# The shift products of five seams in a one-core encoder kernel: 16 matmuls with the shift stationary, the last squares added on VectorE, and the reciprocal root spread at another place

## The reference

```python
def rms_norm(x, gain=None):
    y = x * lax.rsqrt(jnp.mean(x * x, axis=-1, keepdims=True) + EPS)
    return y if gain is None else y * gain
def modulate(h, shift, scale):
    return h * (1 + scale[:, None, :]) + shift[:, None, :]
for i in range(DEPTH):
    mod = cond @ mod_w[i] + mod_b[i]
    sh1, sc1, g1, sh2, sc2, g2, sh3, sc3, g3 = jnp.split(mod, 9, axis=-1)
    x = x + 0.5 * g1 * swiglu(modulate(rms_norm(x), sh1, sc1), ffn1_w_gu[i], ffn1_w_down[i])
    x = x + g2 * mixer(modulate(rms_norm(x), sh2, sc2))
    x = x + 0.5 * g3 * swiglu(modulate(rms_norm(x), sh3, sc3), ffn2_w_gu[i], ffn2_w_down[i])
    x = rms_norm(x, post_gain[i])
```

## Time and profile before

| | us |
|---|---|
| three runs | 2045.1, 2045.5, 2046.54 (median 2045.5) |
| the profiled execution | 2046.44 |
| its span, first to last instruction | 2044.6 |
| PE busy | 2006.3 (98%), 9341 matmul records |
| DVE busy | 1117.0 (55%) |
| ACT busy | 702.6 (34%) |
| POOL busy | 185.3 (9%) |
| mean granted TensorE clock | 0.995 of full |

### The profile page before, as it was taken

The page is one execution under the profiler, slowest core; times in us unless marked ns, Lnnn a source line. Parts: engine busy times, 40 slices in busy tenths (PEclk is TensorE's granted clock), DMA queues, the critical chain, the costliest instruction groups (busy, mean ns, idle before and its releaser), DMA issues.

```text
span 2044.6 us, 23873 instructions
## 1 busy us (share of the span) xinstructions
PE 2006.3 (98%) x9341; PEld 1667.2 (82%) x9341; DVE 1117.0 (55%) x1712; ACT 702.6 (34%) x1025; POOL 185.3 (9%) x216
## 2 busy tenths in 40 slices
PE   6999999999999999999999999999999999999998
PEld 4888888888888888888888888878888888888886
DVE  7664653689757655636763552465455474333334
ACT  5222322454643222225321222345454443222122
POOL 3110100016600101000110000000000000000000
PEclk9999999999999999999999999999999999999999
DMA  8665542322025655623453542221221132322321
GB/s 318 238 209 182 187 146 84 98 86 73 21 91 197 206 173 196 189 85 96 154 196 123 181 139 91 82 94 53 73 72 63 52 93 93 112 92 85 103 87 57
DMA packets 72015, 253.99 MB, mean 124 GB/s; under 512 B 8025, under 2 KB 8153, under 8 KB 71938
## 3 DMA queue, kind: packets, MB, share of 16 engines
q1 hardware_dynamic: 53280, 185.62, 27.9%
q0 software_dynamic: 18512, 67.26, 9.9%
q10 hardware_dynamic: 146, 0.09, 0.0%
HBM read 250.70 MB, written 2.10 MB: 124 GB/s over the span
## 4 chain that ended last, share of the span: by engine, by line
PE 92%; DVE 5%; ACT 1%; issue 1%; POOL 1%; DMA 0%; DVEq 0%; ACTq 0%; SPq 0%; POOLq 0%
PE bank L1244 29%; PE bank L1249 28%; PE bank L1245 28%; PE bank L1308 1%; DVE arena L1067 1%; DVE wlo L711 1%; DVE top L1066 1%; PE bank L1653 1%; PE bank L1695 1%; PE bank L1584 1%; PE bank L1426 1%; ACT whi L397 1%; PE bank L1428 1%; PE bank L1427 1%; PE bank L1641 0%
## 5 line engine op out<-in xcount | busy, mean ns | idle before, releaser
L1244 PE MATMUL bank<-h_hi,whi 128*128 128x512 f32 x1808 | 720.6, 399 | 9.0 <-DVE wlo L711 4.7
L1245 PE MATMUL bank<-h_hi,wlo 128*128 128x512 f32 x1808 | 708.3, 392 | 0.0
L1249 PE MATMUL bank<-h_lo,whi 128*128 128x512 f32 x1808 | 596.0, 392 | 1.7 <-DVE h_lo L828 1.2
L397 ACT ACTIVATE whi<-wraw 128x1024 fp32r<-128x1024 f32 x338 | 347.2, 1054 | 266.9 <-PE bank L1249 263.9
L711 DVE TENSOR_TENSOR wlo<-wraw,whi 128x1024 fp32r<-128x1024 f32 x325 | 390.5, 1224 | 55.0 <-ACT whi L397 53.6
L1244 PEld LDWEIGHTS bank<-h_hi,whi 128*128 128x128 f32 x1808 | 342.5, 189 | 79.1 <-issue 5.6
L1249 PEld LDWEIGHTS bank<-h_lo,whi 128*128 128x128 f32 x1808 | 341.1, 189 | 75.1 <-DVE h_lo L828 2.2
L1245 PEld LDWEIGHTS bank<-h_hi,wlo 128*128 128x128 f32 x1808 | 342.5, 189 | 66.4
L1249 PE MATMUL bank<-hid_lo,whi 128*128 128x512 f32 x832 | 324.7, 390 | 3.2 <-DVE hid_lo L904 3.2
L1244 PE MATMUL bank<-hid_hi,whi 128*128 128x512 f32 x832 | 325.0, 391 | 0.0
L1245 PE MATMUL bank<-hid_hi,wlo 128*128 128x512 f32 x832 | 324.2, 390 | 0.0
(11 more groups left out here) (232 smaller groups left out, 1418.4 us busy)
## 6 DMA issues: line engine op xcount, KB each, us to landing
wraw<-in_w_units_dram SPq DMA_DIRECT2D x306, 512.0 KB, 3.5
arena<-in_mod_t_dram POOLq DMA_DIRECT2D x96, 512.0 KB, 4.8
mod_tile<-in_mod_t_dram POOLq DMA_DIRECT2D x32, 512.0 KB, 4.5
wraw<-in_w_units_dram SPq DMA_DIRECT2D x32, 384.0 KB, 3.3
arena<-in_mod_t_dram SPq DMA_DIRECT2D x12, 512.0 KB, 7.9
xT<-in_xt_dram SPq DMA_DIRECT2D x8, 256.0 KB, 4.8
out_dram<-xT SPq DMA_DIRECT2D x8, 256.0 KB, 2.2
mod_tile<-in_mod_t_dram SPq DMA_DIRECT2D x2, 512.0 KB, 9.6
```

The costliest lines, as they stand in the source:

```text
L397: act.activation(whi[:, s % RING, :, :], wraw[:, s % RING, :, :], ACT.Copy).then_inc(hi_ready, 1)
L1244: pe.matmul(dst, whi[:, w, k, :], hi_, start=first, stop=False)
L1245: pe.matmul(dst, wlo[:, w, k, :], hi_, start=False, stop=False)
L1249: return pe.matmul(dst, whi[:, s % RING, k, :], lo_, start=False, stop=last)
```

## The change

There are four parts.

- The shift products of a seam are taken out of the k loops. `shift_rows` makes them in one piece after k = 6 of unit s: `shift_split[:, k, :]` (2 columns) is stationary, and the 256 weight columns of units s and s+1 stream, 8 k by `whi` and `wlo`, 16 matmuls, into two rows of a bank. DVE copies the two rows to SBUF after k = 1 of `norm`, and `shift_columns` turns them into two columns with two f32 matmuls over 2 partitions after k = 3 of unit s+1. `early_shift` then reads the columns with one copy instead of a copy and an addition.
- DVE also adds the last square (d = 7, at seam 3 the gain's too), so `stat_sums` needs only the matmuls over `ssum`. For this the `lo` of unit s+2 moves behind `var`, that of unit s+3 behind the root's split, and the two last early `h_lo`s behind the addition. At seam 3 the sums come after k = 4.
- The root is spread after k = 5 of unit s; at seam 3 the root that the norm needs (job 7) after k = 7 of unit s, the other after k = 3 of unit s+1. DVE no longer waits for the spread at its end but for `rb_kept` alone. At seam 5 `take_early` and `lo(s + 4)` come after the last tile of `norm` (`late`).
- In DSA, `lo(U + 8)` and the keys' low parts are done by POOL (the latter after its third `hid_lo`), not by DVE.

```diff
-        RB_BEFORE = {1: 2, 2: 3, 3: 5, 4: 6, 5: 7}
+        RB_BEFORE = {1: 2, 2: 3, 3: 4, 4: 6, 5: 7}
...
-            for n in range(9, 12):
+            for n in range(8, 12):
                 lo(DSA_BASE + n)
             job(2, 8)
             for j in range(HEADS):
                 if j == HEADS - 1:
                     job(3, NB * EARLY)
+                if j == 3:
+                    for g in range(KV_HEADS):
+                        pool.wait_ge(qk_rounded, g + 1)
+                        pool.tensor_tensor(qk[:, 2 + g, :], dsa_k[:, g, :], qk[:, g, :].bitcast(F32), ALU.subtract)\
+                            .then_inc(k_ready, 1)
...
-                    act.wait_ge(early_used, KT * (v - 1) + k + 1)
+                    if k < KT - 1:
+                        act.wait_ge(early_used, (KT - 1) * (v - 1) + k + 1)
+                    else:
+                        act.wait_ge(unit_done, s + 2)
...
             def add_sq(st, d):
-                if 1 <= d <= 6:
+                if 1 <= d:
...
-                if st:
+                if st in NORM:
+                    lo(LAST_UNIT[st] - 1)
+                split_roots(j, NB)
+                if st in NORM:
                     lo(LAST_UNIT[st])
-                split_roots(j, NB)
-                dve.wait_ge(rb_ready, st + 1)
+                else:
+                    dve.wait_ge(rb_ready, st + 1)
...
-                lo(LAST_UNIT[3])
+                lo(LAST_UNIT[3] - 1)
                 dve.wait_ge(rstd_ready, NORM_JOB[3] + 1)
...
                 split_roots(NORM_JOB[3], NB)
+                lo(LAST_UNIT[3])
                 dve.wait_ge(rstd_ready, NORM_JOB[4] + 1)
...
                 split_roots(NORM_JOB[4], NB)
-                dve.wait_ge(rb_ready, 5)
...
+                    if k == 1:
+                        dve.wait_ge(rows_done, v)
+                        dve.tensor_copy(sq[0:2, 0, 0:2 * P], bank[SHIFT_BANK][0:2, 0:2 * P]).then_inc(rows_kept, 1)
                     if k:
                         lower(k - 1)
-                    if k == 4:
+                    if k == 4 and not late:
                         lo(s + 4)
-                    if k == 5:
+                    if k == 5 and not late:
                         take_early(s)
                 lower(KT - 1)
+                if late:
+                    take_early(s)
+                    lo(s + 4)
...
-            lo(U + 8)
...
-            top_k(2, 4, 7)
-            for g in range(KV_HEADS):
-                dve.wait_ge(qk_rounded, g + 1)
-                dve.tensor_tensor(qk[:, 2 + g, :], dsa_k[:, g, :], qk[:, g, :].bitcast(F32), ALU.subtract)\
-                    .then_inc(k_ready, 1)
-            top_k(2, 7, 16)
+            top_k(2, 4, 16)
...
+            def shift_rows(s):
+
+                pe.wait_ge(lo_ready, s + 2)
+                w = s % RING
+                rows = bank[SHIFT_BANK][0:2, 0:2 * P].rearrange("p (u n) -> p u n", u=2)
+                for k in range(KT):
+                    for m, weights in enumerate((whi, wlo)):
+                        ins = pe.matmul(rows, shift_split[:, k, :], weights[:, w:w + 2, k, :], start=(k == m == 0),
+                                        stop=(k == KT - 1 and m == 1))
+                ins.then_inc(rows_done, 1)
+
+            def shift_columns(v):
+
+                pe.wait_ge(rows_kept, v)
+                for u in range(2):
+                    pe.matmul(bank[SHIFT_BANK][:, 2 * P + u:2 * P + u + 1], sq[0:2, 0, u * P:(u + 1) * P],
+                              ones[0:2, 0:1], start=(u == 0), stop=True, skip_group_check=True)
...
-                        for m, weights in enumerate((whi, wlo)):
-                            ins = pe.matmul(bank[SHIFT_BANK][:, 2 * q:2 * q + 2], weights[:, w, k, :], shift_split[:, k, :],
-                                            start=(q == k == m == 0), stop=(k == KT - 1 and m == 1), skip_group_check=True)
...
-                        if k == 3 and q == 0:
+                        if q == 0 and k == (4 if st == 3 else 3):
                             stat_sums(st)
-                        if k == 3 and q and st == 3:
-                            pe.wait_ge(root_ready, ROOTS_BEFORE[4] + 1)
-                            spread(bank[RB], NORM_JOB[4], 0).then_inc(rb_ready, 1)
-                    if q == 0:
-                        stat_spread(st, POST_RB if st == 3 else RB)
+                        if q == 0 and k == 5 and st != 3:
+                            stat_spread(RB, ROOTS_BEFORE[st], NORM_JOB[st])
+                        if q == 0 and k == 6:
+                            shift_rows(s)
+                        if q == 0 and k == 7 and st == 3:
+                            stat_spread(RB, ROOTS_BEFORE[4], NORM_JOB[4])
+                        if q and k == 3:
+                            if st == 3:
+                                stat_spread(POST_RB, ROOTS_BEFORE[3], NORM_JOB[3])
+                            shift_columns(v)
```

78 lines of the change are left out of this document (41 added, 37 removed).

## The result

The changed kernel takes 2028.95 us (median of six runs, 2028.07 to 2029.04), the kernel before 2046.01 in the same comparison; the ratio is 0.9912 with a 95% interval of 0.9903 to 0.9922. It is 17.1 us faster. One of the six runs of the kernel before took 8709.12 us, for a reason that no run shows; without it that kernel's median is 2045.5 and the difference 16.6. My forecast was 2035.0, 11.4 us faster; the time lies at the lower end of the range, where rival A (2030) stood, and outside the forecast's own range of 2032 to 2039.

What follows compares the result with a forecast made beforehand. Kernel taken as bound by PE's own work (92% of the chain of waits). 1.7 + 6.8 + 4.1 + 2.0 - 3.2 = 11.4 us off 2046.4 gives 2035.0 (chance 0.53, own range 2032 to 2039); range 2028 to 2042.5.

Steps and rivals of the forecast that it cites:

- rival A: Whole kernel: no slow stretch at a seam and DSA's compare gets in; 16.5 us gained, 2030; chance 0.2.
- Seams 1, 2 and 6: PE's shorter program, less the new wait at the spread: 0.6 us each at 2 and 6, 0.5 at 1.
- Seam 3: Gain 6.8 us, 36.3 to 29.4, mostly from the norm's root leaving unit s+1's middle and the slow stretch going.
- Seam 5: Norm starts 8.2 us behind the seam's start instead of 12.4; PE, waiting for the DVE and ACT chain, gains 4.1.
- 4.2 us sooner ... so this is what PE gets: At seam 5, the norm's earlier start passes through DVE and ACT to PE, which gains 4.1 us.
- DSA: Third compare either runs ahead of POOL's `lo`, gaining 3.9 us, or behind it, gaining 0; middle taken, 2.0.
- The clock: Two slow stretches of PE at the five seams, 1.6 us each: 3.2 us lost, bounds 0 and 8.0.
- the compare's second half: In DSA, the rest of the 3.9 us beyond the 2.0 taken, if the compare gets in: 1.9 us.
- Rival B: Stall at the spread costs the clock at all five seams and DSA's `lo` goes first: 4.6 us, 2042; chance 0.17.
- rival C: Row products at a quarter of the rate, 0.45 us each, at every seam: slower, 2061.4 or 2058; chance 0.05.
- D: DVE's new order bounds seams 3 and 5, only 0.6 us gained per seam: 3.4 us, 2043; chance 0.05.
- the term of 1.3 us: At a seam's early spread, PE arrives 1.45 us behind the sums, the root after 2.77: a new wait of 1.3.

Runs made afterwards that it cites:

- DSA part alone: Kernel before with only `lo(U + 8)` and the keys' low parts moved to POOL (also written before + DSA part); 2042.14 us, ratio 0.9983.
- the seven variants with the same short matmuls: Seven follow-up kernels, each the changed kernel with other edits but its shift products and sums kept; medians from 2022.37 to 2031.99 us.
- the spread behind: Changed kernel with the root's spread back behind unit s (after k = 7) at seams 1, 2, 5 and 6; 2024.71 us, ratio 0.9892.
- DSA part undone: Changed kernel with `lo(U + 8)` and the keys' low parts done by DVE again; 2031.85 us, ratio 0.9932.
- compare late: Changed kernel with two more unused MAX8 on DVE ahead of the third row block's compare in DSA; 2031.99 us, ratio 0.9928.
- rows alone: Kernel before with only the shift products changed to row products, DVE's copy and column matmuls; 2042.04 us, ratio 0.9978.
- not late: Changed kernel with `take_early` and `lo(s + 4)` in the middle of `norm` at seam 5 again; 2029.89 us, ratio 0.9916.
- old products: Changed kernel with the short shift products back in the k loops, row and column products removed; 2033.15 us, ratio 0.9939.

## Why the prediction was right, and where it was off

The time lay inside the range and the direction was right, and most of the mechanism; the sum was 6 us short. What came is rival A, to which I had given 0.2, and not the forecast, to which I had given 0.53. That the range held has luck in it: the stretches of the two traces differ by 18.56 us, 7.2 more than my sum, and from 2046.4 that is 2027.8, under the range's 2028. The profiled execution took 2028.07, with 1.5 us more in its last fillers. Term by term, forecast against the stretches:

- **Seams 1, 2 and 6: 1.7 forecast, 1.79 measured.** Every piece came out within 0.1 us of its price, the stall too (1.14 to 1.18 in the rows, 1.34 from start to start at seam 2, against 1.3).
- **Seam 3: 6.8 forecast, 7.21 measured.** I had put it down mostly to the root's place and the slow stretch. The place is worth 1.10 us net of its stall by its own experiment and the clock 3.3; by my prices PE's shorter program gives the rest (1.06 for the products, 1.79 for 16 records of sums fewer), an estimate that adds up to 7.25. I also read the old seam as bound by PE alone, but PE waited 1.24 us there for the norm's low parts. The norm's start came 11.99 us behind the seam's start (12.45 forecast), the whole from the first matmul to the end of the pair took 991.78 - 962.62 = 29.16 us (29.4 forecast).
- **Seam 5: 4.1 forecast, 5.75 measured, by another way.** The step "4.2 us sooner ... so this is what PE gets" failed. The norm did start at 8.12 us (8.2 forecast), but the first `h_hi` came only 13.26 - 11.48 = 1.78 us sooner, since ACT then waited for PE's unit s+1. I had written down this wait for seam 1 and forgot it at seam 5. What made up for it was the `late` order, which I had counted at nothing: 2.37 us by its own experiment. The other 5.75 - 1.78 - 2.37 = 1.6 us are what is left for the clock, the size of one slow stretch: the one behind the stall of 2.06 us. A second one is inside the 1.78. Behind the sums the clock fell at the old seam 5 and not at the old seam 2, and the first `h_hi` came 13.26 us behind the start in the one and 11.70 in the other; so the sooner spread itself gave `h_hi` only 11.70 - 11.48 = 0.2 us.
- **DSA: 2.0 forecast between 0 and 3.9, 3.81 measured.** The bound was exact and the middle of two discrete cases was the wrong value to take: the compare either gets its place before the `lo` or it doesn't. At the forecast start of 507.5 POOL's `hid_lo` was running until 508.42. No row of before showed who comes next; in each trace in which the compare began during `hid_lo` (the changed kernel and DSA part alone among them) it ran ahead of the `lo`.
- **The clock: -3.2 forecast, 0 measured.** This step failed most. I put in two slow stretches at the seams because two of five had one before; there were none, and none in the seven variants with the same short matmuls. I had named the argument for it (fewer short matmuls) under rival A and held the stall against it; stalls of 0.9 to 1.2 us for the root cost no clock in any of these traces.

Without the clock term my sum is 14.6 us, and with the compare's second half 16.5, which is rival A; 17.1 was measured in the medians, 18.56 in the stretches. Rival B (the stall costs the clock) and rival C (row products at a quarter of the rate) are refuted by the rows, D by seam 3's 7.21 us and by the norm of seam 5 that starts 4.3 us sooner.

What I did not see at all is that the sooner spread is a loss at seams 1, 2 and 6 (1.33 to 1.41 us by the run with the spread behind), with its stall in the term of 1.3 us that I wrote down myself: it buys a norm that nobody waits for. Putting the 16 row products, which are needed later than the root, beside that wait gives 5.8 us more.

## What to carry to other kernels

When a root or another small result is fetched sooner, ask who waits for what follows from it: if the next engine waits for the PE program anyway, the fetch should stand behind independent matmuls that fill its latency. A tiny DVE instruction that lasts as long as POOL's is waiting, not working; where in POOL's sequence it falls decides microseconds. And where a stretch runs at half clock in some traces, look at several traces, and at what stands at that place in each, before you give it a price.

## What the runs showed of the hardware

A DVE compare over 512 columns, SBUF to SBUF, ended 0.28 to 0.29 us behind POOL's tensor_tensor in four traces, for starts 0.28 to 0.61 us into it; issued while one POOL instruction ran, it went ahead of the next, which then lasted 2.58 or 2.59 instead of 2.40 us. Beside POOL's power over 4 or 8 columns nothing was held up: a DVE subtraction over 1024 columns took its 1.22 us, a compare over 256 columns 0.29. MAX8 and MATCH_REPLACE beside POOL's instructions kept their 0.69 and 0.68 us.

A matmul with 2 stationary and 256 streaming columns starts 0.114 to 0.117 us after the one before it in the mean (16 take 1.82 us at seam 2, 1.87 at seam 1), about half of the 0.227 of a 512-column one.

At full clock PE's stalls of 0.9 to 1.2 us for the root were followed by full clock in every trace; behind those of 2.55 to 2.57 us in DSA the clock was at its lower level for a while in each trace that has them (before, DSA part undone, compare late, rows alone), and so it was at the 2.53 us of rows alone at seam 3. Between lies no clean edge: behind stalls of 1.86 us (not late) and 2.07 (before + DSA part) at seam 5 the clock stayed full, at those of 1.87 (rows alone) and 2.06 (before) and at the one of 2.21 (old products, seam 3) it fell. The eight filler matmuls at the kernel's end last 3.32 to 3.76 us in five traces and 2.10 or 2.11 in the other eight, with the same code; so one execution can't tell the last 1.5 us of a difference.
